# Attention with selected keys: scores by key, maxima from one-pass scores, and 32 unread products ahead of a wait

## The reference

```python
sc = jnp.einsum('bkgqd,bkcd->bkgqc', qn, k_cmp).astype(jnp.float32) * scale
p_cmp = masked_softmax(sc, cmp_end[None, :] <= t[:, None])
o_cmp = jnp.einsum('bkgqc,bkcd->bkgqd', p_cmp.astype(v_cmp.dtype), v_cmp)
...
ss = jnp.einsum('bkgqd,bkqnd->bkgqn', qr, ks).astype(jnp.float32) * scale
p_s = masked_softmax(ss, (kpos <= t[:, None])[:, :, None])
o_slc = jnp.einsum('bkgqn,bkqnd->bkgqd', p_s.astype(vs.dtype), vs)
...
o_win = jnp.einsum('bkgqn,bknd->bkgqd', p_w.astype(vw.dtype), vw)
o = gb[0][..., None] * o_cmp + gb[1][..., None] * o_slc + gb[2][..., None] * o_win
```

## Time and profile before

| | us |
|---|---|
| median of 3 runs (lowest, highest) | 4584.19 (4584.19, 4590.88) |
| the profiled run | 4587.89 |
| its span, first to last instruction | 4585.9 |
| PE busy in the span | 4225.6 (92%) |
| DVE, ACT, POOL busy | 2751.3, 1656.5, 600.6 |
| mean granted clock of TensorE over the span | 0.929 |

### The profile page before, as it was taken

How to read it: one execution, slowest core, us unless ns; L and a number is a source line. 1 busy time by engine, 2 the same in 40 slices (tenths; PEclk the granted TensorE clock), 3 DMA queues, 4 the chain that set the end, 5 groups by cost and what they waited for, 6 DMA issues and landing times. The chain is left out here.

```text
span 4585.9 us, 59885 instructions
## 1 busy us (share of the span) xinstructions
PE 4225.6 (92%) x20457; PEld 3602.1 (79%) x20457; DVE 2751.3 (60%) x5213; ACT 1656.5 (36%) x2459; POOL 600.6 (13%) x570
## 2 busy tenths in 40 slices
PE   7999998998999989997989999974888999999998
PEld 6887777777788878877878888742788999988887
DVE  6634654754563366345554332386699788778887
ACT  3222334335322232233444232233333555633333
POOL 1100000000010001002110000000000445333332
PEclk9999999999999999995566999986999999999999
DMA  7622210210463256221001222210234898899997
GB/s 269 224 106 101 92 46 32 74 64 26 171 220 111 95 181 228 101 71 38 1 1 46 78 97 101 74 47 28 86 116 136 317 335 334 308 347 354 355 352 286
DMA packets 136292, 693.07 MB, mean 151 GB/s; under 512 B 15890, under 2 KB 17104, under 8 KB 91088
## 3 DMA queue, kind: packets, MB, share of 16 engines
q1 hardware_dynamic: 63888, 420.62, 25.5%
q0 software_dynamic: 72256, 270.57, 16.1%
HBM read 633.42 MB, written 57.70 MB: 151 GB/s over the span
## 5 line engine op out<-in xcount | busy, mean ns | idle before, releaser
L112 DVE TENSOR_TENSOR w_lo<-raw,w_hi 128x2048 fp32r<-128x2048 f32 x331 | 758.4, 2291 | 703.0 <-ACT w_hi L104 698.7
L124 PE MATMUL ps<-x_hi,w_hi 128*128 128x512 f32 (+1 forms) x2896 | 1097.6, 379 | 84.6 <-DVE w_lo L112 49.8
L125 PE MATMUL ps<-x_lo,w_hi 128*128 128x512 f32 (+1 forms) x2896 | 1082.6, 374 | 0.0
L126 PE MATMUL ps<-x_hi,w_lo 128*128 128x512 f32 (+1 forms) x2896 | 1082.0, 374 | 0.0
L104 ACT ACTIVATE w_hi<-raw 128x2048 fp32r<-128x2048 f32 x331 | 632.7, 1911 | 667.7 <-PE ps L126 439.1
L124 PEld LDWEIGHTS ps<-x_hi,w_hi 128*128 128x128 f32 x2896 | 551.8, 191 | 173.9 <-issue 60.3
L126 PEld LDWEIGHTS ps<-x_hi,w_lo 128*128 128x128 f32 x2896 | 551.0, 190 | 76.6
L125 PEld LDWEIGHTS ps<-x_lo,w_hi 128*128 128x128 f32 x2896 | 552.0, 191 | 73.8
L2013 POOL DMA_INDIRECT ph_rows<-in_peer_u,ph_names x128 | 227.3, 1776 | 638.3 <-DVE ph_names L2373 376.2
L133 PE MATMUL ps<-w_hi,x_hi 128*128 128x512 f32 (+1 forms) x704 | 275.6, 391 | 27.8 <-DVE dp_t L671 17.8
L2096 PE MATMUL ps<-w_hi,px_gh 128*128 128x512 f32 x768 | 299.0, 389 | 1.9 <-issue 1.5
(11 more groups left out here) (355 smaller groups left out, 6326.7 us busy)
## 6 DMA issues: line engine op xcount, KB each, us to landing
raw<-in_slabs SPq DMA_DIRECT2D x331, 1024.0 KB, 4.9
ada_ring<-in_w_ada POOLq DMA_DIRECT2D x160, 512.0 KB, 5.5
act_dram<-px_act SPq DMA_DIRECT2D x64, 384.0 KB
gate_dram<-ps_g SPq DMA_DIRECT2D x12, 2048.0 KB, 12.4
px_g<-gate_dram POOLq DMA_DIRECT2D x32, 768.0 KB, 8.2
px_ai<-act_dram POOLq DMA_DIRECT2D x64, 384.0 KB, 6.5
h_dram<-h SPq DMA_DIRECT2D x2, 2048.0 KB, 8.0
h<-h_dram SPq DMA_DIRECT2D x2, 2048.0 KB, 7.7
```

The lines of the kernel that those rows point to most:

```text
L112: nc.vector.tensor_tensor(k.wlo[:, c % 2, :], k.raw[:, c % 2, :], k.whi[:, c % 2, :].bitcast(F32), ALU.subtract).then_inc(k.raw_free, 1)
L124: mm(out, hi, rhs_hi, start=start, stop=False)
L125: mm(out, hi, rhs_lo, start=False, stop=False)
L126: return mm(out, lo, rhs_hi, start=False, stop=stop)
```

## The change

The attention stage is written anew. Heads are handled one after the other in straight code, with nine items in each: j = 0 for the compressed keys and j = 1 to 8 for the four blocks of 128 in each of the two branches.

- `by_query(h, j)`: scores with the queries on the partitions, from the rounded key part alone (one product where there were two; j = 0 is four products with 32 columns). DVE takes the maxima from them (`maxima`), the masked values go to `junk` and are not used again. `negative` clamps and negates a head's 12 maxima.
- `rows(h)`: PE transposes the negated maxima to 3 rows of 512, ACT copies them to `mrow`.
- `by_key(h, j)`: scores with the keys on the partitions, in both key parts, for all queries from the key block on; to them PE adds the row of maxima (a product with 3 rows, `pick` times `mrow`) and the mask of the block on the diagonal (`ident` times `diag`), for j = 0 the whole mask. ACT takes the exponential from PSUM straight to SBUF (`exps`).
- `values(h, j)`: as before in count and type, without a transpose ahead of it, with a column of ones beside the values (`vo`, `vco`), so that the sum of the exponentials comes out as column 65.
- `output(h)`: all 12 quotients and 768 elements of a head at once, in the midst of the maxima of head h+3.
- By_query runs two heads ahead of by_key; the first two heads' are made ahead of the loop.
- `keep_warm`: 32 products of 512 columns into PSUM bank 0 ahead of PE's wait for `klo`; nothing reads them.
- POOL makes 16 splits of 512 elements where it made 16 of 1024; two more masks are loaded.

The two score banks of by_query are 0 and 1, those of by_key 2 and 3, and the outputs stand in 4 to 7.

```diff
+def keep_warm(k, pe, n, b):
+    for _ in range(n):
+        k.nc.tensor.matmul(bank(k, b), k.xh[:, 0, 0:P], k.xh[:, 0, :], start=True, stop=True)
...
+        def item(h, j):
+            return 1 + 10 * h + j + (j > 2 and h < NH - 1)
...
         @blk.tensor
+            def by_query(h, j):
+                u = 9 * h + j
+                if j == 0:
+                    pe.wait_ge(s["staged"], h + 1)
+                if u > 1:
+                    pe.wait_ge(s["maxed"], u - 1)
...
+                    last = nc.tensor.matmul(bank(k, u % 2, n), qs[:, h % 4, 1, b * P:(b + 1) * P], kk[:, 0, at:at + n],
+                                            start=True, stop=True)
+                last.then_inc(s["s"], 1)
...
+            def by_key(h, j):
+                q = item(h, j)
+                pe.wait_ge(s["act"], max(q - 1, row_item(h) + 1))
...
+                    for part in range(2):
+                        nc.tensor.matmul(bank(k, 2 + q % 2, n), kk[:, part, at:at + P], qs[:, h % 4, 1, kb * P:T],
+                                         start=part == 0, stop=False)
+                    nc.tensor.matmul(bank(k, 2 + q % 2, n), pick[:, 1 + (j - 1) // 4, :], mrow[:, h % 2, kb * P:T],
+                                     start=False, stop=False)
+                    last = nc.tensor.matmul(bank(k, 2 + q % 2, P), ident[:], diag[:], start=False, stop=True)
+                last.then_inc(s["st"], 1)
...
+            keep_warm(k, pe, 32, 0)
             pe.wait_ge(s["klo"], 1)
-            with pe.Fori(0, 4) as jp:
...
-                for u in range(U):
-                    if u < U - 2:
-                        scores(u + 2)
-                    transposes(u)
-                    if u > 0:
-                        values(u - 1)
-                values(U - 1)
+            for h in range(2):
+                for j in range(9):
+                    by_query(h, j)
+            rows(0)
+            pe.wait_ge(s["consts"], 1)
+            pe.wait_ge(s["vo"], 1)
+            by_key(0, 0)
+            for h in range(NH):
+                for j in range(9):
+                    if j == 2 and h < NH - 1:
+                        rows(h + 1)
+                    if j < 8:
+                        by_key(h, j + 1)
+                    elif h < NH - 1:
+                        by_key(h + 1, 0)
+                    if h < NH - 2:
+                        by_query(h + 2, j)
+                    values(h, j)
...
         @blk.scalar
+            def exps(h, j):
+                q = item(h, j)
+                u = 9 * h + j
+                act.wait_ge(s["st"], q + 1)
+                if u > 2:
+                    act.wait_ge(s["pv"], u - 2)
...
         @blk.vector
+            for h in range(NH):
+                for j in range(9):
+                    if j == 4 and h > 0:
+                        output(h - 1)
+                    if h < NH - 2:
+                        maxima(h + 2, j)
```

More of the change, by code:

```diff
@@ L1263, in stage_attend_nsa @@
         o = k.h[:].rearrange("p k t -> p (k t)").rearrange("p (r n) -> p r n", r=NB)
[L1264 removed]
+        s = signals(k, ctx, "na_", ("const", "kpad", "khi", "klo", "vo", "consts", "qhi", "staged", "s", "cadd", "maxed", "neg",
+                                    "st", "act", "pv", "den", "rden", "w", "free", "o"))
         blk = ctx.enter_context(nc.Block(no_gpsimd_drain=True))
[L1267 to L1271, removed]
@@ L1276, in _ @@
         @blk.sync
         def _(sp):
-            sp.dma_start(causal[:], d["mask_causal"]).then_inc(s["const"], 16)
-            sp.dma_start(mcmp[:], d["mask_cmp"]).then_inc(s["const"], 16)
+            for dst, src in ((causal[:], "mask_causal"), (mcmp[:], "mask_cmp"), (raw_diag, "mask_diagT"), (raw_cmp, "mask_cmpT")):
+                sp.dma_start(dst, d[src]).then_inc(s["const"], 16)
         @blk.gpsimd
         def _(gp):
[L1283 to L1293, removed]
@@ new lines, in by_query @@
+            def by_query(h, j):
[4 more added lines that the diff above has]
+                    pe.wait_ge(s["maxed"], u - 1)
+                if j == 0:
+                    for b in range(NB):
+                        last = nc.tensor.matmul(bank(k, u % 2, 32, 32 * b), qs[:, h % 4, 0, b * P:(b + 1) * P],
+                                                kc[:, 0, 32 * kv_of(h):32 * kv_of(h) + 32], start=True, stop=True)
+                else:
+                    at, b = keys_at(h, j)
+                    n = (b + 1) * P
+                    last = nc.tensor.matmul(bank(k, u % 2, n), qs[:, h % 4, 1, b * P:(b + 1) * P], kk[:, 0, at:at + n],
+                                            start=True, stop=True)
+                last.then_inc(s["s"], 1)
@@ new lines, in values @@
+            def values(h, j):
+                pe.wait_ge(s["act"], item(h, j) + 1)
+                slot = (9 * h + j) % 3
+                if j == 0:
+                    if h > 1:
+                        pe.wait_ge(s["free"], h - 1)
+                    for b in range(NB):
+                        last = nc.tensor.matmul(out_at(h, b, 0), pt[0:NC, slot, b * P:(b + 1) * P], vco[:, kv_of(h), :],
+                                                start=b % 2 == 0, stop=False)
+                else:
+                    kb, i = (j - 1) % 4, (j - 1) // 4
+                    for b in range(kb, NB):
+                        last = nc.tensor.matmul(out_at(h, b, 1 + i), pt[:, slot, (b - kb) * P:(b - kb + 1) * P],
+                                                vo[:, i, kb, kv_of(h), :], start=False, stop=i == 1 and kb == b and b % 2 == 1)
+                last.then_inc(s["pv"], 1)
@@ L1383, in _ @@
             V.tensor_copy(kcp[:, :, 0:NC], kcT[:]).then_inc(s["kpad"], 1)
+            V.memset(vo[:, :, :, :, HD:W], 1.0)
+            V.memset(vco[:, :, HD:W], 1.0)
+            V.tensor_copy(vco[:, :, 0:HD], vc[:])
+            for i in range(2):
+                last = V.tensor_copy(vo[:, i, :, :, 0:HD], vn[:, i].rearrange("p b (v d) -> p b v d", v=2))
+            last.then_inc(s["vo"], 1)
             ve.wait_ge(s["khi"], 1)
@@ L1434, in stage_nsa @@
+            ve.wait_ge(s["const"], 64)
+            for h in range(2):
+                for j in range(9):
+                    maxima(h, j)
+                negative(h)
+            for h in range(NH):
+                for j in range(9):
+                    if j == 4 and h > 0:
+                        output(h - 1)
+                    if h < NH - 2:
+                        maxima(h + 2, j)
+                if h < NH - 2:
+                    negative(h + 2)
+            output(NH - 1)
 def stage_nsa(k, d, norm, gate):
```

226 lines of the change are left out of this document (119 added, 107 removed).

## The result

| | median us | lowest to highest | runs |
|---|---|---|---|
| before | 4587.28 | 4584.19 to 4590.88 | 4 |
| after | 4708.38 | 4700.81 to 4713.19 | 4 |

The changed kernel takes 1.0261 of the time of the kernel before, 95% interval 1.0246 to 1.0275: 121 us slower, where the prediction had 4443 us and a range from 4425 to 4490. The profiled execution has a span of 4704.5 us.

A forecast was written before the change was run, and what follows sets the result against it. The attention stage was taken as PE work at half clock. 14 heads x 12.9 + 2 x 11.2 = 203 us, stalls 10 and 3 for slow first products put its end 141 us earlier: 4443 us, range 4425 to 4490.

The forecast's parts named there:

- The clock: Attention loop: TensorE's clock rises to 2.4 GHz in the first head and stays, so a head costs 12.9 us.
- The rival that named this: Attention stage: clock stays at 1.2 GHz, value records and 3- or 31-row products weighing against it; 4621 us; chance 6%.
- The price of a head at 1.2 GHz: PE's records in one new attention head, counted at the lower clock: 24.9 us.
- Its test against the length of a pass: Old attention loop: four heads counted at 1.2 GHz give 86.6 us, beside a 6 us stop, for a 93 us pass.
- The stall behind DVE's output: Attention loop: PE waits for a maximum behind the output, 0.7 to 0.8 us in 13 heads, 10 us.
- PE's own work: Attention loop: PE's records in one new head at 2.4 GHz take 12.9 us.
- The output: DVE's output of an attention head, in one piece between two maxima, takes 2.8 us.
- The head of the stage: Attention stage's start: key split ends when it did, first scores about 2121, both first heads' maxima take 11.5 us.
- The first exponential: Attention stage's start: the first exponential comes at about 2135.
- The 32 products: Unread products before the key wait: end between 2117.5 and 2124.7; cost nothing if the clock rises, 4 us if never.
- POOL's passes: POOL's query splits in the attention loop: half as large for each of 16 heads, and away from the output.
- The signs: Attention stage: granted clock 0.9 or more; 13.6 us between heads, or 25 at the lower clock.

The follow-up runs named there:

- e1: The changed kernel with the products that add the maxima padded by zeros from 3 to 128 rows: 4453.13 us, 0.9703 of the kernel before.
- e2: The changed kernel without eight of the nine 3-row products of each head: 4478.29 us.
- e12: e1 with its 32 unread products on 3 rows instead of 128: 4457.03 us in one run.
- e4: The changed kernel without the 32 unread products: 4707.24 us, 1.027 of the kernel before.
- e9: e1 with a product of 3 rows and 4 columns added ahead of eight padded products in each head: 4675.53 us in one run.
- e8: e1 with 3 rows again in the products of the second branch, four a head: 4470.38 us in one run.

## Why the prediction was wrong

**The clock** is the step that failed, by its sentence "I take it that the clock rises in the first head and stays". It counted records by their columns: eight of 512 close together, 20 of 100 wide. The score pairs in front of the old loop's rises all had 128 rows, and so had the records priced in the earlier trace rows. Of the 20 wide records of the new head, five (the products that add the maxima, over 512 and 384 columns, and that of the compressed keys) have 3 rows and one has 31. What the runs showed in its place: with these products on 3 rows the clock stood at 0.50 in head after head (29.85 us each), with the same on 128 rows at 1.00 (13.86, e1). The other half of the sentence, that nothing leaves PE idle for more than a microsecond, didn't help: it looked at PE's waits, and not at the half microsecond that each of these products costs beside its columns (e2). The rival that named this had 6%, together with the value records, which don't hold the clock down by themselves (e1). A 3-row product stands in no row of the trace before, and deserved more doubt than that.

**The price of a head at 1.2 GHz** failed too, 24.9 against 29.85: this is why the rival's 4621 us was 87 short as well, 79 of them from this (16 x 4.95). The weight load was taken as hidden for every form, because it was for all in the earlier trace rows. But the kernel before had a form for which it wasn't, the value records of the compressed keys on 31 rows, as a timeline near its end shows:

```profile
2483.72 0.42 PE L1319 MATMUL ps<-ident,na_sm 128*128 128x128 f32 x1
2484.07 0.50 PEld L1332 LDWEIGHTS ps<-nsa_vc,na_pt 31*128 31x128 f32 x2 [0.33 <-issue]
2484.07 0.69 PE L1332 MATMUL ps<-nsa_vc,na_pt 31*128 31x64 f32 x2
2484.69 1.22 PE L1310 MATMUL ps<-na_k,na_q 128*128 128x512 f32 x2
```

The transpose takes 0.35 us to the next start in place of 0.21, and the two records 0.62 in place of 0.42. Four such places in a head are 1.4 us, and an old head at 0.50 took 23.2 us (512-column pairs of successive heads start at 2250.61, 2273.86 and 2297.02) where the prediction counted 21.6. Its test against the length of a pass, 86.6 and 6 for 93, came out by luck: a pass ran in part at the upper clock, so it should have come out shorter than a count at 1.2 GHz.

The Trainium skill ("TensorEngine Tiling (Array Packing)", Key Properties) says that TensorE is drained where the tiling mode changes. The Trainium skill ("TensorEngine Tiling (Array Packing)", Available Configurations) lists modes with 128, 64 and 32 rows. The trace is as this rule would have it if a product on few rows counts as another mode: PEld idles 0.65 us ahead of the 3-row load, and not at all between the 3-row loads of e12. That it does count as one is a reading that no run here shows.

So of the 265 us between forecast and result 256 are the stage (500.66 for 244.9). By head: 13.65 forecast with its stall, 29.85 measured. Of the 16.2 between them 12.0 are the lower clock by the prediction's own count (24.9 less 12.9), 4.95 are what a head took beyond that count (4.2 of them the eight standstills, by e2), and the stall of 0.75 fell away.

**What held**, and can be seen in e1, which is the changed kernel as the prediction imagined it. Its stage took 249.05 us for the 244.9 forecast, and a head 13.86 for 13.6. That it comes so near is luck in part, as two misses nearly cancel. The stall behind DVE's output is 0.27 us a head, not 0.7 to 0.8, as the waits of its weight loads in thirteen heads of e1 show:

```profile
PEld ps L1330 <- DVE na_mx L1462: 3.5, 13, 0.3
```

And PE's own work is 13.6, not 12.9. The output took 2.7 us (2618.95 to 2621.65) for 2.8. The head of the stage was late: first scores 13.1 us after its begin, not 11.4. Two of DVE's splits, one of them with 64 elements only, take 3.14 and 2.30 us beside a POOL pass of 4.29; in the kernel before they took 2.27 and 0.96, and the long pass began with the last split. e4 has the same 3.12 and 2.27, so it isn't the 32 products. The first exponential starts after 29.0 us (2150.39) instead of 25.4. The 32 products ended 3.5 us before the wait, with the clock up after their first third, and cost nothing. POOL's passes are not half as large, as the change and the prediction had them: they still have 1024 elements and take 1.2 and 2.5 us, and hid all the same.

**The signs** named beforehand pointed right: a stage clock of 0.51 instead of 0.9 and 25 us or more between heads were what "the clock stays" should show.

What stays open: how the low clock of the changed kernel divides between the standstill and the columns on few rows. Each was shown with little or nothing of the other (e9; e12), the one left the clock at 0.54, the other at 0.50, and the changed kernel has both. How many 3-row products it takes is known only within bounds: four a head left the clock at 1.00 (e8), eight tiny ones didn't (e9). The 31-row products were not tried apart, nor was a standstill without a product on few rows.

## What to carry to other kernels

When a product is added for a small operand (a row of maxima, a bias, a one-hot pick), look at the rows its weights fill, not only at its columns: pad them with zeros to 128 rows where it stands among 128-row products. Here the filled product took no more time than the 3-row one, and the filling was worth 255 us (4708.38 less 4453.13). Between 64 and 128 rows nothing was measured. When pricing a stream that should run at the upper clock, don't take products on few rows as work that will raise it, and look at PEld's idle time and at the starts, since PE's busy share says 99 to 100% in either case.

## What the hardware showed that I had not expected

- The clock and the rows: 32 products of 512 columns on 3 or 64 rows stay at 0.50 for 13.9 us; on 128 rows they reach 1.00 after some 3 us and are done in 8.8 to 8.9.
- A change between rows puts two weight loads in the open: 0.53 us for a 3-row product among 128-row ones at 1.2 GHz, 0.27 at 2.4. With 64 rows it is the same as with 3 (heads of 29.85 us in both).
- Leaving work out can be slower: e2, with eight products fewer, is 25 us slower than e1, since its clock falls in every second head.
